# Scores of two attention branches: the second precision pass on 64 rows per head, heads paired on row halves and banks

## The chip, the cores and the metric

The kernel runs on one core of a Trainium2 chip. The metric is the time of one execution on the device in microseconds (us), as a median over runs. Durations inside the kernel come from one profiled execution.

## What is computed

One layer of a hybrid backbone for 256 prompt tokens and 1024 latent tokens on a 16 x 64 grid. A combined projection feeds two attention branches, whose outputs are gated, projected, merged and projected again. Cut to what the change touches:

```python
# branch A: 8 heads x 64, neighbourhood window 8 x 16 on the grid, learned bias, plus 512 context keys
s_nb  = jnp.einsum('brjqhd,brjkhd->brjhqk', qg, kb).astype(jnp.float32) * ATTN_SCALE + bias[None]
s_ctx = jnp.einsum('brjqhd,bshd->brjhqs', qg, ck).astype(jnp.float32) * ATTN_SCALE
p = _softmax_f32(jnp.concatenate([s_nb, s_ctx], axis=-1)).astype(v.dtype)
o = (jnp.einsum('brjhqk,brjkhd->brjqhd', p[..., :nk], vb)
     + jnp.einsum('brjhqs,bshd->brjqhd', p[..., nk:], cv))
# branch B: 8 query heads on 2 key heads, window of 128 tokens each way, a sink logit, the same context keys
p = _softmax_f32(jnp.concatenate([s_nb, s_ctx, sink_col], axis=-1))[..., :-1].astype(v.dtype)
```

## The kernel before, in words

**Stages.** First the norm, modulation, keys and values (to about 137 us), then branch A (to about 575 us), branch B (to about 968 us), then the branch and output projections.

**Precision.** Every product of two float32 operands is made from fast float32r matmuls on operands split into a high and a low part: high x high, high x low, low x high. A head has 64 channels and the array has 128 rows, so a score needs two passes. In the first, `q1` holds the high part of the query in both halves of the rows, and `kk` (projected keys) or `kc` (context keys) holds the high part of the key in one half and the low part in the other: one 128-row matmul gives two of the three products. In the second pass, `q2` holds the low part of the query in the half where that head's high key lies (rows 0 to 63 for the first head of a pair, 64 to 127 for the second).

**Steps.** Each branch runs four pairs of heads. A pair has 9 steps, `STEPS`: step 0 for the 256 prompt tokens of both heads, and steps 1 to 8, each with two score tiles `t` of 128 queries against 512 context keys and 2 or 3 blocks of 128 near keys (2 at the first and last tile of the grid, 3 within; "edge" and "interior" below). In branch B the tiles of a step are the same 128 queries for both heads. In branch A before, they are two neighbouring tiles of one head (`tile_of`), four steps for each head; on each tile the kernel multiplies on 128 rows in both passes, with the other half of `q2` set to zero by GpSimd.

**One step.** TensorE writes the scores to `s_ps` (four banks: two for each `t`), VectorE takes minima and adds the bias (`minima`), ScalarE takes the exponentials, VectorE normalises. TensorE then transposes the probabilities in chunks of up to four blocks (`transposes`, into `t_ps`), ScalarE and VectorE split them into high and low parts `pt`, and TensorE weights the values (`weighted`, into `o_ps`): half 0 on the context values `vc`, half 1 on the near values `vw`. The value block is the stationary operand, and the columns that move are the queries. In one step of a single head, both tiles move through one loading of a value block: 256 columns, where both tiles see the block. ScalarE's `low_half` and VectorE's `add_halves` then combine the halves into `ost`.

**Order.** TensorE's order is written out by hand. In turn s of a pair it makes the scores of step s, the near half of `weighted` for step s-2, two transpose chunks of step s-1, one gate projection `unit` (24 matmuls into `d_ps`), the other transposes of s-1, and the context half of `weighted` for s-1.

**Tiling of the array.** The kernel names no tile of the array: a matmul on operands of 64 rows occupies the row half in which its operands lie.

Of the kernel before, what the change touches and what calls it, by code (L numbers as in the profile page):

```python
# [41 lines left out]
P = 128  # L42
# [32 lines left out]
CHUNKS = {"a": [2] + [4] * SAMPLES, "b": [2, 3] + [4] * (SAMPLES - 2) + [3]}  # L75
NCHUNK = {b: sum(n) for b, n in CHUNKS.items()}
CHUNKS_ALL = PAIRS * (NCHUNK["a"] + NCHUNK["b"])

# [631 lines left out]
def pairs(nc, io, block, hm, ident, wt, wraw, craw, w_in, w_hi, w_lo, tiles, own, counts, earlier_stage, branch, f=None):  # L710
# [61 lines left out]
    if A:  # L772
        comb_in = [sem("comb_in0"), sem("comb_in1")]
        ko_done, ko_out, q2_zero = (sem(n) for n in ("ko_done", "ko_out", "q2_zero"))
# [14 lines left out]

    chunks = CHUNKS[branch]  # L790
    chunk0 = [sum(chunks[:s]) for s in range(STEPS)]

    def chunk_base(p):

        return (0 if A else PAIRS * NCHUNK["a"]) + p * NCHUNK[branch]

# [10 lines left out]
    def tile_of(s, t):  # L807

        return 2 * ((s - 1) % 4) + t if A else s - 1

    def near0(s, t):

        return max(tile_of(s, t) - 1, 0)

    def near_n(s, t):

        return min(tile_of(s, t) + 2, BLOCKS) - near0(s, t)

    def near_bank(s, t):
        w = near_n(s, t) * P  # L820
        return s_ps[:, 2 * t, PAST - w:PAST] if s % 2 else s_ps[:, 2 * t + 1, 0:w]

    def scores_run(s, t):

        w = near_n(s, t) * P
# [3 lines left out]
    def probs_run(s, t):  # L829
        w = near_n(s, t) * P  # L830
# [10 lines left out]
    def probs_block(s, t, kb):  # L841

        c0 = NB + kb * P if kb < 4 or s % 2 == 0 else NB + (kb - 4 - near_n(s, t)) * P
        return pr[:, t, c0:c0 + P]

    def shared(s):

        ends = [(near0(s, t), near0(s, t) + near_n(s, t)) for t in range(2)]
        return [(b, [t for t in range(2) if ends[t][0] <= b < ends[t][1]]) for b in range(ends[0][0], ends[1][1])]

    def chunk_blocks(s):
# [5 lines left out]
        near = [(4 + b - near0(s, t), t) for b, ts in shared(s) for t in ts]  # L857
# [17 lines left out]
    def _(sp):  # L875
# [6 lines left out]
        def body(p, last):  # L882
# [22 lines left out]
            def load_bias(h):  # L905
# [14 lines left out]
            if A:  # L920
                for done, count in stored:
                    sp.wait_ge(done, count)
                load_bias(0)
                load_bias(1)
# [25 lines left out]

    @block.gpsimd
    def _(pool):
        if not A:
            return
        for done, count in stored:
            pool.wait_ge(done, count)
        for h in range(2):
            r1 = HD * (1 - h)
            pool.memset(q2[r1:r1 + HD, h, :].bitcast(F32), 0.0).then_inc(q2_zero, 1)
            pool.wait_ge(q2_zero, h + 1)  # L960

    @block.tensor
    def _(pe):
        def body(p, last):
# [29 lines left out]
            def score(s, t, out, rhs, head=None):  # L994

                if s == 0:
                    h, q0 = head, LAT + t * P
                elif A:
                    h, q0 = (s - 1) // 4, tile_of(s, t) * P
                else:  # L1000
                    h, q0 = t, tile_of(s, t) * P
                cols = lambda ap: ap[..., q0:q0 + P]
                pe.matmul(out, cols(q1[:, h, :]), rhs(h, slice(0, P)), start=True, stop=False)  # L1003
                return pe.matmul(out, cols(q2[:, h, :]), rhs(h, slice(0, P)), start=False, stop=True)  # L1004

            def scores(s):
                if s == 0:
                    if A:
                        pe.wait_ge(q2_zero, 2)
# [12 lines left out]
                for t in range(2):  # L1022
                    if s == 0:
                        for head in range(2):
                            mm = score(s, t, prompt_scores(t, head), lambda h, r: kk[r, h, LAT:TOK], head)
                        continue
                    score(s, t, s_ps[:, 2 * t + s % 2, :], lambda h, r: kc[r, h, :])
                    near = slice(near0(s, t) * P, (near0(s, t) + near_n(s, t)) * P)
                    mm = score(s, t, near_bank(s, t), lambda h, r: kk[r, h, near])
                mm.then_inc(s_done, 1)  # L1030

            def transposes(s, c):

                n = chunk0[s] + c
# [8 lines left out]
            def weighted(s, half):  # L1043
# [5 lines left out]
                last_chunk = chunks[s] if half else 2  # L1049
                pe.wait_ge(lo_done, chunk_base(p) + chunk0[s] + last_chunk)  # L1050
# [8 lines left out]
                elif half == 0:  # L1059
                    h = (s - 1) // 4 if A else 0  # L1060
                    work = [(vc[:, kb, h, :], 2 * kb, 0, 2) for kb in range(4)]
                else:
                    h = (s - 1) // 4 if A else 0
                    work, b0 = [], 8
                    for b, ts in shared(s):
                        work.append((vw[:, b, h * P:(h + 1) * P], b0, ts[0], len(ts)))
                        b0 += len(ts)
# [15 lines left out]
            for s in range(STEPS + 1):  # L1083
# [6 lines left out]
                if s > 0:  # L1090
                    for c in range(min(2, chunks[s - 1])):
# [5 lines left out]
                if s > 0:  # L1097
                    for c in range(2, chunks[s - 1]):
# [7 lines left out]
    def _(act):  # L1106
# [6 lines left out]
        def body(p, last):  # L1113
# [45 lines left out]
            def high(s, chunks):  # L1159

                for c in chunks:
                    n = chunk0[s] + c
# [10 lines left out]
            def exps(s):  # L1173
                for t in range(2):
                    n = pb * 2 * STEPS + 2 * s + t + 1
                    act.wait_ge(m_done, n)
                    if t == 0:

                        act.wait_ge(t_done, chunk_base(p) + (chunk0[s - 1] + min(2, chunks[s - 1]) if s > 0 else 0))
                        act.wait_ge(r_done, pb * STEPS + s)  # L1180
                    if s == 0:
                        for h in range(2):
                            c = 2 * t + h
# [75 lines left out]
            for s in range(STEPS + 1):  # L1259
# [4 lines left out]
                if s > 0:  # L1264
                    high(s - 1, range(min(2, chunks[s - 1])))
# [6 lines left out]
                if s > 0:  # L1272
                    high(s - 1, range(2, chunks[s - 1]))
# [29 lines left out]
    def _(dve):  # L1303
# [7 lines left out]
        def body(p, last):  # L1311
# [83 lines left out]
            def low(s, chunks):  # L1395

                for c in chunks:
                    n = chunk0[s] + c
# [5 lines left out]
            def minima(s):  # L1404
# [4 lines left out]
                if A:  # L1409
                    h = (s - 1) // 4  # L1410
                    dve.wait_ge(comb_in[h], (p + 1) * 16)
# [8 lines left out]
                for t in range(2):  # L1420
                    b = tile_of(s, t)
                    if A:
                        c0 = 0 if 0 < b < BLOCKS - 1 else NB if b == 0 else NB + EDGE
                        near = comb[:, h, c0:c0 + near_n(s, t) * P]
                    else:
                        c0 = P if b == 0 else 0
                        near = band[:, c0:c0 + near_n(s, t) * P]
# [4 lines left out]
            def prompt_minima():  # L1432
# [4 lines left out]
                both = s_ps[:, :, :].rearrange("p (t b) (h c) -> p t b h c", b=2, h=2)[:, :, 0, :, :]  # L1437
                grid4 = lambda ap: ap[:, :].rearrange("p (t h) -> p t h", h=2)
# [6 lines left out]
                sk = nsk[:, :].rearrange("p (o h) -> p o h", o=1).to_broadcast([P, 2, 2])  # L1445
                dve.tensor_tensor(grid4(mx), grid4(mn), sk, ALU.min).then_inc(m_done, 2)

            def normalise(s):
# [13 lines left out]
                for t in range(2):  # L1462
                    if s == 0:
                        for h in range(2):
                            c = 2 * t + h
# [25 lines left out]
            def add_halves(s):  # L1491
# [10 lines left out]
                elif A:  # L1502
                    h, j = (s - 1) // 4, (s - 1) % 4
                    dst = grid(ost[HD * h:HD * h + HD, :], 0, ROWS, 2 * CW * j, 2 * CW).rearrange("p r (t c) -> p t r c", t=2)
                    dve.tensor_tensor(dst, o_ps[0:HD, 0:2 * P].rearrange("p (t r c) -> p t r c", t=2, c=CW),
# [625 lines left out]
```

## Time and profile before

| | |
|---|---|
| median of 3 runs | 1214.7 us (1214.63 to 1215.92) |
| the profiled execution | 1216.12 us, its span 1214.3 us |
| TensorE (PE) busy | 1188.0 us, 98% of the span |
| VectorE (DVE), ScalarE (ACT), GpSimd (POOL) busy | 817.1, 599.9 and 92.9 us |
| granted TensorE clock, mean | 0.997 |

PE stands for TensorE's matmuls and PEld for its weight loads, which run beside them. A matmul's recorded length goes past the moment at which the next may start; the distance from one start to the next is what it costs in a stream. A row of several matmuls gives the first start and the length to the last end. "x128" is a count of instructions, `128*128` the active rows and columns of the array, and `128x256` partitions by moving columns. In this trace `L1003` and `L1004` are the first and second pass of the scores, `L1070` is `weighted`, `L1040` the transposes, `L84` the split projections.

### The profile page before, as it was taken

Reading aid. Unit: us, or ns where it says so; the run is one execution under the profiler, and the core shown is the slowest. Engines: PE = TensorE matmul, PEld = TensorE weight load, DVE = VectorE, ACT = ScalarE, POOL = GpSimd, SP = SyncE. Lnnn points to the kernel's source line nnn. Section 1 sums busy time; section 2 is a strip of 40 time slices with the busy share of each in tenths; the row PEclk is TensorE's granted clock in tenths of the full one; section 3 lists DMA queues with packets and bytes.
Section 4 is the critical chain, followed back from the end, with each engine's and each line's share of the span. In section 5 each row is a group of like instructions: output and inputs, shape, how many; then the busy total and the mean of one; then the engine's idle time right before and its main releaser. Section 6 shows DMA issues by size and latency. Waiting matters only on the chain.

```text
span 1214.3 us, 19600 instructions
## 1 busy us (share of the span) xinstructions
PE 1188.0 (98%) x7408; PEld 1075.5 (89%) x7408; DVE 817.1 (67%) x1588; ACT 599.9 (49%) x1200; POOL 92.9 (8%) x108
## 2 busy tenths in 40 slices
PE   7999999999999999999999999999999999999997
PEld 1799889989998999899899899989989988998995
DVE  4769458656765776587687687688779876354352
ACT  4632335535552654365465455556547675344341
POOL 0000000000000000000000000000000034533430
PEclk9999999999999999999999999999999999999999
DMA  9447702141123215022411111411113376642630
GB/s 362 171 180 225 239 22 72 45 135 61 40 80 95 64 40 159 25 72 77 130 63 47 49 64 39 133 39 58 42 39 121 118 245 193 216 158 76 219 127 35
DMA packets 71617, 132.80 MB, mean 109 GB/s; under 512 B 6758, under 2 KB 47718, under 8 KB 71532
## 3 DMA queue, kind: packets, MB, share of 16 engines
q1 hardware_dynamic: 57420, 109.96, 28.0%
q10 hardware_dynamic: 14112, 21.70, 4.9%
q8 instruction: 54, 0.88, 0.3%
q14 instruction: 31, 0.25, 0.1%
HBM read 96.24 MB, written 35.40 MB: 108 GB/s over the span
## 4 chain that ended last, share of the span: by engine, by line
PE 85%; DVE 9%; ACT 3%; issue 2%; DMA 1%; POOL 0%; ACTq 0%; SPq 0%; DVEq 0%
PE d_ps_pairs L84 23%; PE s_ps_pairs L84 12%; PE y_ps L1858 9%; PE b_ps L84 9%; PE o_ps_pairs L1070 9%; PE t_ps_pairs L1040 7%; PE v_ps L84 6%; PE s_ps_pairs L1004 4%; PE s_ps_pairs L1003 4%; DMA wada<-in_w_ada 1%; DVE pt L1401 1%; PE k_ps L352 1%; DVE mn L1407 1%; DVE q L1392 1%; PE t_ps L344 1%
## 5 line engine op out<-in xcount | busy, mean ns | idle before, releaser
L84 PE MATMUL d_ps_pairs<-h,wt 128*128 128x384 f32 (+2 forms) x1920 | 352.2, 338 | 0.9 <-ACT craw L1212 0.9
L84 PEld LDWEIGHTS d_ps_pairs<-h,wt 128*128 128x128 f32 x1920 | 316.7, 189 | 16.4 <-ACT craw L1212 1.9
L1401 DVE TENSOR_TENSOR pt<-t_ps_pairs,pt 128x512 fp32r<-128x512 f32 (+2 forms) x264 | 152.9, 619 | 64.7 <-ACT pt L1170 63.4
L84 PE MATMUL s_ps_pairs<-h,wt 128*128 128x512 f32 (+1 forms) x864 | 168.2, 354 | 0.0
L84 PEld LDWEIGHTS s_ps_pairs<-h,wt 128*128 128x128 f32 x864 | 141.6, 189 | 21.7
L1170 ACT ACTIVATE pt<-t_ps_pairs 128x512 fp32r<-128x512 f32 (+2 forms) x264 | 130.2, 544 | 16.9 <-PE t_ps_pairs L1040 11.5
L1194 ACT ACTIVATE pr<-s_ps_pairs,mx 128x896 f32<-128x896 f32 (+1 forms) x128 | 125.1, 982 | 26.9 <-DVE mx L1429 26.5
L1040 PE MATMUL t_ps_pairs<-ident_sb,pr 128*128 128x128 f32 x928 | 125.6, 274 | 1.9 <-DVE pt L1401 1.1
L1858 PE MATMUL y_ps<-wo,mg 128*128 128x512 f32 x480 | 113.2, 396 | 0.0
L1040 PEld LDWEIGHTS t_ps_pairs<-ident_sb,pr 128*128 128x128 f32 x928 | 105.4, 140 | 8.7 <-DVE pt L1401 5.7
L1858 PEld LDWEIGHTS y_ps<-wo,mg 128*128 128x128 f32 x480 | 90.0, 188 | 21.6 <-POOL mg L1815 0.2
L1407 DVE TENSOR_REDUCE mn<-s_ps_pairs 128x2 f32<-128x1024 f32 x64 | 78.1, 1221 | 39.5 <-PE s_ps_pairs L1004 39.4
L1812 POOL TENSOR_TENSOR tp<-tp 128x256 f32<-128x256 f32 x40 | 33.2, 829 | 889.3 <-DVE tp L1910 888.9
L1212 ACT ACTIVATE craw<-d_ps_pairs 128x384 f32<-128x384 f32 (+2 forms) x80 | 39.2, 489 | 106.1 <-PE d_ps_pairs L84 105.7
L84 PE MATMUL b_ps<-og,wb 128*128 128x256 f32 x720 | 87.7, 282 | 1.6 <-DVE tp L1910 1.6
L84 PEld LDWEIGHTS b_ps<-og,wb 128*128 128x128 f32 x720 | 86.8, 188 | 2.1 <-DVE wb L1587 1.0
L1244 ACT ACTIVATE otmp<-o_ps_pairs 64x256 f32<-64x256 f32 (+1 forms) x72 | 29.2, 406 | 109.1 <-PE o_ps_pairs L1070 108.6
L1470 DVE TENSOR_SCALAR pr<-pr,rden 128x896 f32<-128x896 f32 (+1 forms) x128 | 80.0, 667 | 2.3
L84 PE MATMUL v_ps<-wv,h 128*128 128x320 f32 x456 | 69.6, 310 | 0.0
L84 PEld LDWEIGHTS v_ps<-wv,h 128*128 128x128 f32 x456 | 67.1, 188 | 1.0 <-issue 0.9
L1910 DVE TENSOR_TENSOR tp<-b_ps,gt 128x256 f32<-128x256 f32 x80 | 31.8, 419 | 45.7 <-PE b_ps L84 31.2
L1003 PE MATMUL s_ps_pairs<-kc,q 128*128 128x512 f32 x128 | 50.5, 394 | 0.0
(192 smaller groups left out, 1584.8 us busy)
## 6 DMA issues: line engine op xcount, KB each, us to landing
wraw<-in_w_gate SPq DMA_DIRECT2D x24, 512.0 KB, 3.9
gt<-gates_d SPq DMA_DIRECT2D x40, 256.0 KB, 4.5
gates_d<-craw ACTq DMA_DIRECT2D x48, 192.0 KB, 1.9
v_d<-vst SPq DMA_DIRECT2D x20, 320.0 KB, 4.5
wada<-in_w_ada SPq DMA_DIRECT2D x12, 512.0 KB, 9.6
oz<-gates_d SPq DMA_DIRECT2D x20, 256.0 KB, 4.6
oz<-o_d SPq DMA_DIRECT2D x20, 256.0 KB, 4.2
x_f<-in_x SPq DMA_DIRECT2D x10, 512.0 KB, 6.3
```

Of the source, the lines that this page charges most:

```text
L84: mm = eng.matmul(out, lhs(a, k), rhs(b, k), start=(k == 0 and i == 0), stop=(k == n_k - 1 and i == 2))
L1003: pe.matmul(out, cols(q1[:, h, :]), rhs(h, slice(0, P)), start=True, stop=False)
L1004: return pe.matmul(out, cols(q2[:, h, :]), rhs(h, slice(0, P)), start=False, stop=True)
L1040: mm = pe.transpose(t_ps[:, n % 2, b * P:(b + 1) * P], probs_block(s, t, kb), ident[:, :])
L1070: mm = pe.matmul(o_ps[:, c0 * P:(c0 + nb) * P], v, pt[:, part, b0 * P:(b0 + nb) * P], start=(half == 0 and part == 0 and (n == 0 or (s == ...
L1170: act.activation(pt[:, 0, c * 512:c * 512 + cols], t_ps[:, n % 2, 0:cols], ACT.Copy).then_inc(hi_done, 1)
L1194: act.activation(probs_run(s, t), scores_run(s, t), ACT.Exp, bias=mx[:, t:t + 1], scale=-1.0, accum_out=den[:, t:t + 1]).then_inc(exp_done, 1)
L1212: act.activation(gst[:, u % 2, 0:n], d_ps[:, 0:n], ACT.Copy).then_inc(g_done, 1)
L1401: dve.tensor_tensor(pt[:, 1, c * 512:c * 512 + cols], t_ps[:, n % 2, 0:cols], pt[:, 0, c * 512:c * 512 + cols].bitcast(F32), ALU.subtract) ...
L1407: dve.tensor_reduce(mn[:, 0:2], s_ps[:, :, :].rearrange("p (t b) c -> p t b c", b=2)[:, :, s % 2, :], AX.X, ALU.min).then_inc(m1_done, 1)
L1470: dve.tensor_scalar(probs_run(s, t), probs_run(s, t), rden[:, t:t + 1], None, ALU.mult).then_inc(p_done, 1)
L1858: mm = pe.matmul(y_ps[:, e, n * 512:(n + 1) * 512], mg[:, a, k, e * P:(e + 1) * P], wo[k][:, b, n * 512:(n + 1) * 512], start=(k == 0 and ...
```

## The change

- The second pass of a score is a matmul on 64 rows: the half of `q2` and of the keys in which that head's data lie. The zero fill of `q2` is gone.
- A step of branch A is now one tile of 128 queries for both heads, as in branch B, so `t` is the head in both branches. In a step the first passes of all four products come first, then the four second passes, alternating between the heads, hence between row halves and banks. In step 0 the banks are those of the heads.
- `weighted` of branch A: a step has two heads, each with its own values, so a value block serves 128 columns, not 256. The number of score columns, transposed blocks and weighted columns is unchanged.
- Chunks of branch A are now as those of B (3 in the edge steps, 4 in the others; before, 4 in all, some of one block).
- The bias of both heads comes in one DMA, waited for as one; `add_halves` of branch A is two instructions of 64x128, not one of 64x256; a GpSimd memset of the last stage waits for branch A's first pair.

```diff
-CHUNKS = {"a": [2] + [4] * SAMPLES, "b": [2, 3] + [4] * (SAMPLES - 2) + [3]}
+CHUNKS = [2, 3] + [4] * (SAMPLES - 2) + [3]
...
-    def near0(s, t):
-        return max(tile_of(s, t) - 1, 0)
+    def near0(s):
+        return max(s - 2, 0)
...
-        return s_ps[:, 2 * t, h * PROMPT:(h + 1) * PROMPT]
+        return s_ps[:, 2 * h, t * PROMPT:(t + 1) * PROMPT]
...
-                sp.dma_start(comb[:, h, :], io["bias"][2 * p + h]).then_inc(comb_in[h], 16)
+                sp.dma_start(comb[:, :, :], io["bias"][2 * p:2 * p + 2].rearrange("h p c -> p h c")).then_inc(comb_in, 16)
...
-            pool.memset(q2[r1:r1 + HD, h, :].bitcast(F32), 0.0).then_inc(q2_zero, 1)
...
-                pe.matmul(out, cols(q1[:, h, :]), rhs(h, slice(0, P)), start=True, stop=False)
-                return pe.matmul(out, cols(q2[:, h, :]), rhs(h, slice(0, P)), start=False, stop=True)
+                h, q0 = (head, LAT + t * P) if s == 0 else (t, (s - 1) * P)
+                if part == 0:
+                    return pe.matmul(out, q1[:, h, q0:q0 + P], k[:, h], start=(s > 0 or t == 0), stop=False,
+                                     skip_group_check=(s == 0))
+                r = slice(h * HD, (h + 1) * HD)
+                return pe.matmul(out, q2[r, h, q0:q0 + P], k[r, h], start=False, stop=True, skip_group_check=(s == 0))
...
+                    for part in range(2):
+                        for t in range(2):
+                            score(s, t, s_ps[:, 2 * t + s % 2, :], kc[:, :, :], part)
+                        for t in range(2):
+                            mm = score(s, t, near_bank(s, t), kk[:, :, near], part)
...
-                elif half == 0:
-                    h = (s - 1) // 4 if A else 0
-                    work = [(vc[:, kb, h, :], 2 * kb, 0, 2) for kb in range(4)]
+                elif A:
+                    near = [vw[:, near0(s) + b, :] for b in range(near_n(s))]
+                    both = near if half else [vc[:, kb, :, :].rearrange("p h c -> p (h c)") for kb in range(4)]
+                    work = [(v[:, t * P:(t + 1) * P], 8 * half + 2 * b + t, t, 1) for b, v in enumerate(both) for t in range(2)]
...
+        pool.wait_ge(exp_done, 2 * STEPS)
         pool.memset(epsc[:, 0:1], EPS).then_inc(eps_set, 1)
```

TensorE in branch A, first pair, from the context half of `weighted` of one step to the transposes of the next, before:

```order
L1070 MATMUL o_ps_pairs<-pt,vc_a 128x256 x8
L1003 MATMUL s_ps_pairs<-kc,q 128x512
L1004 MATMUL s_ps_pairs<-kc,q 128x512
L1003 MATMUL s_ps_pairs<-kk,q 128x384
L1004 MATMUL s_ps_pairs<-kk,q 128x384
L1003 MATMUL s_ps_pairs<-kc,q 128x512
L1004 MATMUL s_ps_pairs<-kc,q 128x512
L1003 MATMUL s_ps_pairs<-kk,q 128x256
L1004 MATMUL s_ps_pairs<-kk,q 128x256
L1070 MATMUL o_ps_pairs<-pt,vw_a 128x128 x2
L1070 MATMUL o_ps_pairs<-pt,vw_a 128x256 x4
L1070 MATMUL o_ps_pairs<-pt,vw_a 128x128 x2
```

and the same place now (`L973` is the first pass, `L976` the second, `L1043` is `weighted`; the rows of `L976` are on 64 rows of the array, which this view does not print):

```order
L1043 MATMUL o_ps_pairs<-pt,vc_a 128x128 x16
L973 MATMUL s_ps_pairs<-kc,q 128x512 x2
L973 MATMUL s_ps_pairs<-kk,q 128x384 x2
L976 MATMUL s_ps_pairs<-kc,q 128x512 x2
L976 MATMUL s_ps_pairs<-kk,q 128x384 x2
L1043 MATMUL o_ps_pairs<-pt,vw_a 128x128 x12
```

The second passes moved behind all first passes, and `weighted` went from 16 matmuls to 28 in such a step. In branch B, TensorE before:

```order
L1070 MATMUL o_ps_pairs<-pt,vc_b 128x256 x8
L1003 MATMUL s_ps_pairs<-kc,q 128x512
L1004 MATMUL s_ps_pairs<-kc,q 128x512
L1003 MATMUL s_ps_pairs<-kk,q 128x384
L1004 MATMUL s_ps_pairs<-kk,q 128x384
```

and now:

```order
L1043 MATMUL o_ps_pairs<-pt,vc_b 128x256 x8
L973 MATMUL s_ps_pairs<-kc,q 128x512 x2
L973 MATMUL s_ps_pairs<-kk,q 128x384 x2
L976 MATMUL s_ps_pairs<-kc,q 128x512 x2
L976 MATMUL s_ps_pairs<-kk,q 128x384 x2
```

Here only the order of the passes moved (before, the four rows of a tile came twice), and `weighted` is as it was.

## Rows read from the trace of the kernel before

**Rows 1.** The page: busy time by engine, and the chain that ended last

```profile
PE 1188.0 (98%) x7408; PEld 1075.5 (89%) x7408; DVE 817.1 (67%) x1588; ACT 599.9 (49%) x1200; POOL 92.9 (8%) x108
PE 85%; DVE 9%; ACT 3%; issue 2%; DMA 1%; POOL 0%; ACTq 0%; SPq 0%; DVEq 0%
```

**Rows 2.** Windows of branch A and branch B: length, busy by engine, clock, DMA

```profile
137.00:575.00 438.00, 437.05 (x2740) 405.15 (x2740) 297.82 (x569) 213.34 (x436) 2.43 (x3) 1.00 0.24 76
575.00:968.00 393.00, 388.50 (x2450) 359.14 (x2449) 306.50 (x675) 226.16 (x509) 0.00 (x0) 1.00 0.23 72
```

**Rows 3.** Waits of TensorE: for whom, us in total, times, longest

```profile
PE o_ps_pairs L1070 <- DVE ost L1510: 2.1, 4, 0.5
...
PE o_ps_pairs L1070 <- DVE ost L1505: 0.8, 4, 0.2
```

**Rows 4.** Timeline of TensorE, one step of branch A: start, length, work, count

```profile
417.95 1.19 PE L1070 MATMUL o_ps_pairs<-pt,vc_a 128*128 128x256 f32 x8
418.98 0.39 PE L1003 MATMUL s_ps_pairs<-kc,q 128*128 128x512 f32 x1
419.21 0.39 PE L1004 MATMUL s_ps_pairs<-kc,q 128*128 128x512 f32 x1
419.44 0.33 PE L1003 MATMUL s_ps_pairs<-kk,q 128*128 128x384 f32 x1
419.61 0.34 PE L1004 MATMUL s_ps_pairs<-kk,q 128*128 128x384 f32 x1
...
420.25 0.28 PE L1003 MATMUL s_ps_pairs<-kk,q 128*128 128x256 f32 x1
420.37 0.28 PE L1004 MATMUL s_ps_pairs<-kk,q 128*128 128x256 f32 x1
420.48 1.04 PE L1070 MATMUL o_ps_pairs<-pt,vw_a 128*128 128x128 f32 x8
421.36 1.06 PE L1040 MATMUL t_ps_pairs<-ident_sb,pr 128*128 128x128 f32 x8
```

**Rows 5.** The same timeline one step earlier, near half of an edge step

```profile
411.64 0.82 PE L1070 MATMUL o_ps_pairs<-pt,vw_a 128*128 128x256 f32 x6
412.30 1.06 PE L1040 MATMUL t_ps_pairs<-ident_sb,pr 128*128 128x128 f32 x8
```

**Rows 6.** TensorE's groups by shape: count, busy us, mean ns

```profile
L1040 PE MATMUL t_ps_pairs<-ident_sb,pr 128*128 128x128 f32 x928 | 125.6, 274 | 1.9 <-DVE pt L1401 1.1
...
L1004 PE MATMUL s_ps_pairs<-kc,q 128*128 128x512 f32 x128 | 50.4, 394 | 0.0
...
L1004 PE MATMUL s_ps_pairs<-kk,q 128*128 128x384 f32 x96 | 32.5, 338 | 0.0
...
L1004 PE MATMUL s_ps_pairs<-kk,q 128*128 128x256 f32 x64 | 17.0, 282 | 0.0
...
L1070 PE MATMUL o_ps_pairs<-pt,vw_a 128*128 128x128 f32 x96 | 16.9, 257 | 0.0
...
L333 PE MATMUL mod_ps<-ident_sb,h 4*128 4x4 f32 x16 | 1.5, 202 | 0.2 <-DVE h L664 0.2
```

**Rows 7.** Timeline of TensorE where it goes between 128 and 4 rows

```profile
34.42 0.60 PE L344 MATMUL t_ps<-ident_sb,x 128*128 128x128 f32 x4
34.95 0.41 PE L333 MATMUL mod_ps<-ident_sb,h 4*128 4x4 f32 x4
35.58 0.41 PE L333 MATMUL mod_ps<-ident_sb,h 4*128 4x4 f32 x4 [0.22 <-DVE h L664]
35.92 0.66 PE L344 MATMUL t_ps<-ident_sb,x 128*128 128x128 f32 x4
```

**Rows 8.** Window of one branch A step from transposes to transposes: TensorE busy first

```profile
421.36:430.41 9.05, 9.05 (x64) 8.85 (x64) 6.99 (x15) 5.60 (x11) 0.00 (x0) 1.00 0.06 23
```

**Rows 9.** Timeline of VectorE in that step: the normalisation

```profile
425.21 1.22 DVE L1470 TENSOR_SCALAR pr<-pr,rden 128x896 f32<-128x896 f32 x2
```

**Rows 10.** DMA issues: the bias, count, size, median us to landing

```profile
comb_a<-in_bias SPq DMA_DIRECT2D x8, 448.0 KB, 6.5
```

More of the change, by code:

```diff
@@ L74 @@
 SAMPLES = STEPS - 1
-CHUNKS = {"a": [2] + [4] * SAMPLES, "b": [2, 3] + [4] * (SAMPLES - 2) + [3]}
-NCHUNK = {b: sum(n) for b, n in CHUNKS.items()}
-CHUNKS_ALL = PAIRS * (NCHUNK["a"] + NCHUNK["b"])
+CHUNKS = [2, 3] + [4] * (SAMPLES - 2) + [3]
+CHUNK0 = [sum(CHUNKS[:s]) for s in range(STEPS)]
+NCHUNK = sum(CHUNKS)
 def split_mm(eng, out, lhs, rhs, n_k):
@@ L788, in grid @@
         return ap[..., 0:LAT].rearrange("p (r c) -> p r c", c=GRID_W)[:, r0:r0 + nr, c0:c0 + ncol]
-    chunks = CHUNKS[branch]
-    chunk0 = [sum(chunks[:s]) for s in range(STEPS)]
     def chunk_base(p):
-        return (0 if A else PAIRS * NCHUNK["a"]) + p * NCHUNK[branch]
+        return (p + base) * NCHUNK
     def rows(ap, g):
@@ L841, in probs_block @@
     def probs_block(s, t, kb):
-        c0 = NB + kb * P if kb < 4 or s % 2 == 0 else NB + (kb - 4 - near_n(s, t)) * P
+        c0 = NB + kb * P if kb < 4 or s % 2 == 0 else NB + (kb - 4 - near_n(s)) * P
         return pr[:, t, c0:c0 + P]
-    def shared(s):
-        ends = [(near0(s, t), near0(s, t) + near_n(s, t)) for t in range(2)]
-        return [(b, [t for t in range(2) if ends[t][0] <= b < ends[t][1]]) for b in range(ends[0][0], ends[1][1])]
     def chunk_blocks(s):
@@ L856, in chunk_blocks @@
             return [[(2 * h + kb, t) for h in range(2) for t in range(2)] for kb in range(2)]
-        near = [(4 + b - near0(s, t), t) for b, ts in shared(s) for t in ts]
+        near = [(4 + b, t) for b in range(near_n(s)) for t in (0, 1)]
         ctx_ = [(kb, t) for kb in range(4) for t in (0, 1)]
@@ L1021, in scores @@
                     pe.wait_ge(exp_done, pb * 2 * STEPS + 2 * s)
[L1022 to L1029, printed above, removed]
+                near = slice(near0(s) * P, (near0(s) + near_n(s)) * P) if s > 0 else slice(LAT, TOK)
+                if s == 0:
+                    for part in range(2):
+                        for t in range(2):
+                            for head in range(2):
+                                mm = score(s, t, prompt_scores(t, head), kk[:, :, near], part, head)
+                else:
+                    for part in range(2):
+                        for t in range(2):
+                            score(s, t, s_ps[:, 2 * t + s % 2, :], kc[:, :, :], part)
+                        for t in range(2):
+                            mm = score(s, t, near_bank(s, t), kk[:, :, near], part)
                 mm.then_inc(s_done, 1)
             def transposes(s, c):
-                n = chunk0[s] + c
+                n = CHUNK0[s] + c
                 if c == 0:
@@ L1058, in weighted @@
                     work = [(vp[:, kb, 0:P], 4 * kb, 0, 4) for kb in range(2)]
-                elif half == 0:
-                    h = (s - 1) // 4 if A else 0
-                    work = [(vc[:, kb, h, :], 2 * kb, 0, 2) for kb in range(4)]
-                else:
[L1063 to L1067, printed above, removed]
+                elif A:
+                    near = [vw[:, near0(s) + b, :] for b in range(near_n(s))]
+                    both = near if half else [vc[:, kb, :, :].rearrange("p h c -> p (h c)") for kb in range(4)]
+                    work = [(v[:, t * P:(t + 1) * P], 8 * half + 2 * b + t, t, 1) for b, v in enumerate(both) for t in range(2)]
+                else:
+                    near = [vw[:, near0(s) + b, :] for b in range(near_n(s))]
+                    both = near if half else [vc[:, kb, 0, :] for kb in range(4)]
+                    work = [(v, 8 * half + 2 * b, 0, 2) for b, v in enumerate(both)]
                 for n, (v, b0, c0, nb) in enumerate(work):
@@ L1090, in body @@
                 if s > 0:
-                    for c in range(min(2, chunks[s - 1])):
+                    for c in range(min(2, CHUNKS[s - 1])):
                         transposes(s - 1, c)
@@ L1097, in body @@
                 if s > 0:
-                    for c in range(2, chunks[s - 1]):
+                    for c in range(2, CHUNKS[s - 1]):
                         transposes(s - 1, c)
```

96 lines of the change are left out of this document (35 added, 61 removed).

## The prediction

> **What bounds the kernel now.** I read the page's busy times first: TensorE is busy 98% of the span, and 85% of the chain that ended last is its own work [rows 1]. Then the windows of the two branches: TensorE works 437.05 of 438.00 us in A and 388.50 of 393.00 in B, at a granted clock of 1.00, while VectorE has 297.82 and 306.50 us of work [rows 2]. Then its waits: the only ones inside the branches that count are for `ost` at the end of a pair, 2.1 us in B and 0.8 in A [rows 3]. So in both branches the end is set by the sum of TensorE's start-to-start distances. What the change adds there is added to the kernel, and what it takes away is a gain until the chain through VectorE and ScalarE shows. That chain has room: in the step shown TensorE is busy for all 9.05 us [rows 8]; the normalisation ends at 425.21 + 1.22 = 426.43 us [rows 9], and TensorE asks for it at 430.41, 4 us later [rows 8].
>
> **Distances.** A matmul of 512 columns takes 419.44 - 419.21 = 0.23 us of the stream, one of 384 takes 0.17, one of 256 takes 0.12 [rows 4]. One of 128 columns is not half of that: eight transposes last 1.06, the last one 0.27 of it [rows 4, 6], so (1.06 - 0.27) / 7 = 0.113 between starts; other such groups give 0.10 to 0.11. The weighted near values say the same: eight matmuls, four of 128 and four of 256 columns, in 421.36 - 420.48 = 0.88 us [rows 4], less 4 x 0.12 leaves 0.10 for each narrow one. In the edge step, six, of which two are narrow, take 0.66 [rows 5], which leaves 0.09. I take 0.11, with 0.10 and 0.113 as bounds: every matmul brings a load of 128 weight columns, and below 256 moving columns the load seems to be what is seen.
>
> **Branch A's weighted values, TensorE.** Before, each of the 32 steps with samples has a context half of 418.98 - 417.95 = 1.03 us [rows 4] and a near half, 0.88 in half of the steps [rows 4] and 0.66 in the other half [rows 5]: 32 x 1.03 + 16 x 0.88 + 16 x 0.66 = 57.6 us. After, all are narrow: 16 for each context half (512), 12 for a near half in 24 steps and 8 in 8 edge steps (352), 864 in all where there were 480. 864 x 0.11 = 95.0 us. That is **+37.4 us** (+28.8 at 0.10, +40.0 at 0.113). No other work hides it, since TensorE has no gap in these steps [rows 8].
>
> **The second pass, both branches.** Its matmuls are the x128, x96 and x64 groups [rows 6]: 128 x 0.23 + 96 x 0.17 + 64 x 0.12 = 53.4 us. By step: 0.80 us in the 48 interior ones, 0.70 in the 16 edge ones, 0.48 in the 8 prompt steps. On 64 rows a matmul streams as many columns, so alone it costs the same; a gain comes only if the two heads' matmuls, now in different row halves and banks, run at once. No row of this trace has two matmuls on different row halves. The bounds are therefore no overlap, 0, and full overlap: 0.40, 0.35 and 0.24 saved, 48 x 0.40 + 16 x 0.35 + 8 x 0.24 = 26.7 us. Between them I take overlap with one weight load after the other, 0.11 us each as above: the four matmuls then start at 0, 0.11, 0.22 and 0.33 us, and the last ends its stream 0.17 later, 0.50 us for 0.80 (edge 0.45 for 0.70, prompt 0.45 for 0.48). That saves 48 x 0.30 + 16 x 0.25 + 8 x 0.03 = **-18.6 us**.
>
> A rule bears on it: the Trainium skill, TensorE: Matmul & The Clock Gate, Part 3, says that matmuls in different row groups run concurrently and gives 3.07 times the rate for four row tiles at 512 columns. No run here shows it. By that efficiency (0.77 of the ideal) two tiles would save about 17 us of the second pass, an estimate from that page.
>
> **Changing between 128 and 64 rows.** Each of the 72 steps goes from 128 rows to 64 and back, 144 changes. The nearest rows are the 4-row transposes of the modulation [rows 7]. The group at 35.58 has its last matmul at 35.58 + 0.41 - 0.20 = 35.79 (mean length 0.20 [rows 6]). The 128-row group behind it is recorded at 35.92 and lasts 0.66 where the like group at 34.42 lasts 0.60, so it really starts near 35.98, 0.19 after. Normal distances are 0.07 (4 rows) and 0.11 (128), which leaves 0.08 to 0.12 for the change. The other way, from the last matmul of the group at 34.42 (34.75) to 34.95 is 0.20, 0.09 above normal, with a wait beside it. I take 0.11: **+15.8 us**. Bounds: 0, and a full wait, the part of a matmul that now overlaps the next (0.39 - 0.23 = 0.16 [rows 4]) and a load not made ahead (0.11), 0.27 or 39 us.
>
> The Trainium skill, TensorEngine Tiling (Array Packing), Key Properties, says that changing the tiling mode drains TensorE, while changing tiles within a mode does not. Rows 7 agree with some such cost. It is the rule that speaks against this change: a step pays for two drains to pair two rather short products.
>
> **Edits at nothing.** VectorE's second `add_halves` instruction (32 of about 0.2 us in branch A) lies in the 4 us of room. The bias in one DMA: its two transfers land in 6.5 us each [rows 10] and are issued at the end of the pair before, more than 30 us ahead of use, so even both in turn are in time. The same minima and exponentials are taken. The zero fill and the GpSimd wait have nobody behind them. Chunks at the edge: the same 108 blocks a pair. If the room were gone, `add_halves` would cost its 6 us, nothing else.
>
> **Sum.** 37.4 - 18.6 + 15.8 = +34.6 us. On the profiled execution, 1216.1 (span 1214.3), that is 1250.7; the median of the runs is 1.4 lower, so 1249. By stage: in A, 438 us become about 475, of which 37.4 is `weighted` and the rest nearly cancels; in B, 393 stay within 2 us, since an interior step gains 0.30 and pays 0.22.
>
> **The rivals.**
> - *Clean pairs and cheap changes.* The halves overlap fully and a change costs at most 0.04: 37.4 - 26.7 + (0 to 6), 1225 to 1231. For it: weight loads are otherwise hidden behind long matmuls. Against it: rows 7. Chance 0.18.
> - *No real overlap.* The float32r matmuls of two halves run one after the other, so the change doesn't do what it says in the scores, and the row changes are paid: 37.4 + 15.8 to 37.4 + 39, 1268 to 1291. For it: no row shows two matmuls at once. Chance 0.25.
> - *Narrow matmuls are faster than they look, and the kernel ends faster.* The place is `weighted` in branch A. Transposes may be slow for a reason of their own, and the 4-row group goes at 0.07 us with the same 128 weight columns [rows 7]. At 0.06 us, 864 cost 52, which is 6 less than before, and with -18.6 + 15.8 the kernel ends at 1206. With the scores as forecast it decides below (57.6 + 2.8) / 864 = 0.070 us. Against it: the narrow ones in `vw_a` left 0.09 to 0.10. Chance 0.05.
> - *In between*, from 1231 to 1241 or 1259 to 1268: a change at 0.05 or 0.18, pairs partly overlapped, or narrow matmuls at 0.10. Chance 0.12.
>
> On the third: the Trainium skill, TensorE: Matmul & The Clock Gate, Back-to-back issue gap, gives about 81 ns for a sustained pair of load and matmul at 128 columns; by it `weighted` would cost 70 us, an estimate, and the whole about 25 us less than my sum. The measured 0.10 to 0.113 decides against it.
>
> **How the numbers follow.** The forecast, 1241 to 1259, has a chance of 0.40. The range goes from 1225, the floor of clean pairs, to 1276, the part of no overlap in which a change costs up to 0.17: 0.40 + 0.17 + 0.12 + 0.12, about 8 in 10. A measurement of this kernel tells about 0.2% (2.4 us) from no change. Faster is the narrow-matmul rival alone and a combination with clean pairs, 0.06; the same 0.02; slower 0.92.
>
> **What would show it.** In the changed profile: (1) `vc_a` and `vw_a` as 864 matmuls of 128 columns with groups of sixteen in about 1.76 us; 1.0 would mean the third rival. (2) The four second-pass matmuls of an interior step from first start to the next work in 0.50 us plus the changes; two starts within 0.02 us mean clean pairs, 0.23 apart means none. (3) The distance from the last 384-column matmul of the first pass to the first of 64 rows, 0.17 normally, now near 0.28, and the same on the way back. (4) Branch A's stage near 475 us and B's near 393, with no new waits of TensorE above 2 us. The prediction is wrong if B's stage moves by over 5 us either way (then the scores were mis-sized) or if A's moves by under 25.

## The result and the profile after

The changed kernel takes 1256.97 us (median of 4 runs, 1255.74 to 1258.45) where the kernel before takes 1214.78 (1214.63 to 1215.92): ratio 1.0346, 95% interval 1.0328 to 1.0364, 42 us slower. The forecast was 1249, range 1225 to 1276.

The page of the changed kernel, busy times and chain, to be held against [rows 1]:

```profile
PE 1227.8 (98%) x7792; PEld 1088.1 (87%) x7792; DVE 824.3 (66%) x1612; ACT 597.9 (48%) x1192; POOL 90.3 (7%) x106
...
PE 84%; DVE 9%; ACT 3%; issue 2%; DMA 1%; POOL 0%; ACTq 0%; SPq 0%; DVEq 0%
```

TensorE is the bound as before, with 384 more matmuls and 39.8 us more work. Nothing else became one.

Its groups by shape (count, busy us, mean ns), which answer to [rows 6]:

```profile
L1043 PE MATMUL o_ps_pairs<-pt,vc_a 128*128 128x128 f32 x512 | 63.5, 277 | 2.9 <-DVE ost L1480 2.9
...
L1043 PE MATMUL o_ps_pairs<-pt,vw_a 128*128 128x128 f32 x352 | 46.0, 279 | 0.0
...
L976 PE MATMUL s_ps_pairs<-kc,q 64*128 64x512 f32 x128 | 32.0, 495 | 0.0
...
L976 PE MATMUL s_ps_pairs<-kk,q 64*128 64x384 f32 x96 | 16.3, 335 | 0.0
```

The 864 narrow matmuls are there. The second pass on 64 rows is busy 32.0 us on the context keys where it was 50.4, and 16.3 on the near keys where it was 32.5: two matmuls at a time.

The timeline of one interior step of branch A (start, length, work, count), which answers to [rows 4]:

```profile
440.42 1.98 PE L1043 MATMUL o_ps_pairs<-pt,vc_a 128*128 128x128 f32 x16
442.24 0.68 PE L973 MATMUL s_ps_pairs<-kc,q 128*128 128x512 f32 x2
442.76 0.52 PE L973 MATMUL s_ps_pairs<-kk,q 128*128 128x384 f32 x2
443.20 0.50 PE L976 MATMUL s_ps_pairs<-kc,q 64*128 64x512 f32 x2
443.54 0.34 PE L976 MATMUL s_ps_pairs<-kk,q 64*128 64x384 f32 x2
443.81 1.56 PE L1043 MATMUL o_ps_pairs<-pt,vw_a 128*128 128x128 f32 x12
445.20 1.06 PE L1014 MATMUL t_ps_pairs<-ident_sb,pr 128*128 128x128 f32 x8
```

The context half of the weighted values takes 442.24 - 440.42 = 1.82 us where it took 1.03, the near half 1.39 where it took 0.88. Two 64-row matmuls of 512 columns last 0.50 together and two of 384 last 0.34, as long as one: both heads start within 0.01 us. This is clean overlap.

Where the price of the pairing lies is best seen in branch B, whose weighted values did not change. TensorE there in an interior step, matmuls and then weight loads:

```profile
671.36 0.51 PE L973 MATMUL s_ps_pairs<-kk,q 128*128 128x384 f32 x2
671.80 0.50 PE L976 MATMUL s_ps_pairs<-kc,q 64*128 64x512 f32 x2
672.13 0.34 PE L976 MATMUL s_ps_pairs<-kk,q 64*128 64x384 f32 x2
672.40 0.98 PE L1043 MATMUL o_ps_pairs<-pt,vw_b 128*128 128x256 f32 x6
```

```profile
671.14 0.41 PEld L973 LDWEIGHTS s_ps_pairs<-kk,q 128*128 128x128 f32 x2
671.80 0.19 PEld L976 LDWEIGHTS s_ps_pairs<-kc,q 64*128 64x128 f32 x2 [0.25 <-issue]
671.91 0.19 PEld L976 LDWEIGHTS s_ps_pairs<-kk,q 64*128 64x128 f32 x2
672.40 0.77 PEld L1043 LDWEIGHTS o_ps_pairs<-pt,vw_b 128*128 128x128 f32 x6 [0.31 <-issue]
```

The last 128-row matmul starts at 671.36 + 0.51 - 0.34 = 671.53. The first 64-row one is recorded at 671.80 and lasts 0.50 where a 512-column matmul lasts 0.39, so it streams from 671.90: 0.37 after, where 0.17 is normal. The change in costs 0.20. About half of it is the weight load: between matmuls of 128 rows it is made beside the matmul ahead (the two loads of 671.14 to 671.55), here it starts only at 671.80, after 0.25 us without a load. On the way back it is the same: from 672.13 to 672.40, plus 0.10 by which the group of six lasts longer (0.98; six such lasted 0.88 before), 0.37 for 0.17. Between the two pairs there is no loss: 671.90 to 672.13 is 0.23. So an interior step saves 0.40 us by overlap and pays 0.40 for two changes.

A table of the two branches (us), each from the start of its first projection to the start of what follows it, in the timelines of the profiled executions. Before, branch A so taken ends at 583.41 and branch B at 976.67, about 8 us behind the cuts of [rows 2]:

| kernel | A, four pairs | B, four pairs |
|---|---|---|
| before | 446.28 | 393.25 |
| changed | 487.91 | 393.06 |

All of the loss is in branch A: 10.0 us in each of three of its pairs and 11.6 in one. That one holds a dip of the granted clock (pairs 2 to 4: length, busy times, clock 0.99 in the middle row; then the dip alone):

```profile
258.54:380.13 121.59, 120.88 (x798) 109.56 (x798) 77.07 (x150) 53.31 (x108) 0.00 (x0) 1.00 0.22 68
380.13:503.35 123.22, 122.51 (x799) 110.72 (x798) 77.09 (x150) 53.30 (x108) 0.00 (x0) 0.99 0.20 66
503.35:624.91 121.56, 120.85 (x798) 109.51 (x798) 77.09 (x150) 53.31 (x108) 0.00 (x0) 1.00 0.28 87
...
380.13:383.60 3.47, 3.47 (x10) 2.71 (x10) 1.79 (x3) 0.38 (x1) 0.00 (x0) 0.51 0.72 279
```

There TensorE runs at the lower of its two levels, 1.2 GHz, on the first projections of the pair. Ahead of it lies the end of a pair with a wait of 0.71 us, as in the other pairs, which have no dip; why it fell is not shown. The dip costs 1.6 us in this execution, and no other trace of this case has one inside the branches.

The last new thing is a wait. The changed kernel's waits for the combined output, to be held against [rows 3], and the end of a pair in A:

```profile
PE o_ps_pairs L1043 <- DVE ost L1480: 4.9, 8, 0.7
```

```profile
253.12 1.54 PE L1043 MATMUL o_ps_pairs<-pt,vw_a 128*128 128x128 f32 x12
254.49 0.63 PE L1014 MATMUL t_ps_pairs<-ident_sb,pr 128*128 128x128 f32 x4
255.83 1.98 PE L1043 MATMUL o_ps_pairs<-pt,vc_a 128*128 128x128 f32 x16 [0.71 <-DVE ost L1480]
```

Between the near half of step 7 and the context half of step 8 only four transposes are left (five before), while ScalarE copies and VectorE adds the output of step 7: 0.7 us of waiting at each pair end of A where it was 0.2, 2.1 us more in all. Experiments 1 and 3 show how much of that comes from the small edits.

### The profile page after: what moved, and what is told of

It is laid out like the page before. It is cut to its first block, busy times and chain, and to the rows that moved or that the text cites. A ratio compares the mean times of both kernels' runs of the same rounds, so it can differ in the third digit from the quotient of the medians.

```text
span 1255.5 us, 20371 instructions
## 1 busy us (share of the span) xinstructions
PE 1227.8 (98%) x7792; PEld 1088.1 (87%) x7792; DVE 824.3 (66%) x1612; ACT 597.9 (48%) x1192; POOL 90.3 (7%) x106
## 4 chain that ended last, share of the span: by engine, by line
PE 84%; DVE 9%; ACT 3%; issue 2%; DMA 1%; POOL 0%; ACTq 0%; SPq 0%; DVEq 0%
PE d_ps_pairs L84 21%; PE o_ps_pairs L1043 12%; PE s_ps_pairs L84 12%; PE y_ps L1828 9%; PE b_ps L84 9%; PE t_ps_pairs L1014 7%; PE v_ps L84 5%; PE s_ps_pairs L973 4%; PE s_ps_pairs L976 3%; DMA wada<-in_w_ada 1%; DVE mn L1380 1%; PE k_ps L352 1%; ACT pr L1167 1%; DVE pt L1374 1%; DVE q L1365 1%
## 5 line engine op out<-in xcount | busy, mean ns | idle before, releaser
L84 PEld LDWEIGHTS d_ps_pairs<-h,wt 128*128 128x128 f32 x1920 | 316.9, 189 | 15.8 <-ACT craw L1185 1.1
L1374 DVE TENSOR_TENSOR pt<-t_ps_pairs,pt 128x512 fp32r<-128x512 f32 (+1 forms) x256 | 152.6, 635 | 69.1 <-ACT pt L1143 66.4
L84 PE MATMUL s_ps_pairs<-h,wt 128*128 128x512 f32 (+1 forms) x864 | 170.8, 357 | 0.0
L1143 ACT ACTIVATE pt<-t_ps_pairs 128x512 fp32r<-128x512 f32 (+1 forms) x256 | 129.7, 556 | 14.7 <-PE t_ps_pairs L1014 9.3
L1043 PE MATMUL o_ps_pairs<-pt,vc_a 128*128 128x128 f32 x512 | 63.5, 277 | 2.9 <-DVE ost L1480 2.9
L1043 PEld LDWEIGHTS o_ps_pairs<-pt,vc_a 128*128 128x128 f32 x512 | 59.7, 192 | 4.1 <-DVE pt L1374 3.7
```

The source lines that it names most:

```text
L84: mm = eng.matmul(out, lhs(a, k), rhs(b, k), start=(k == 0 and i == 0), stop=(k == n_k - 1 and i == 2))
L1043: mm = pe.matmul(o_ps[:, c0 * P:(c0 + nb) * P], v, pt[:, part, b0 * P:(b0 + nb) * P], start=(half == 0 and part == 0 and (n == 0 or (s == ...
L1143: act.activation(pt[:, 0, c * 512:c * 512 + cols], t_ps[:, n % 2, 0:cols], ACT.Copy).then_inc(hi_done, 1)
L1374: dve.tensor_tensor(pt[:, 1, c * 512:c * 512 + cols], t_ps[:, n % 2, 0:cols], pt[:, 0, c * 512:c * 512 + cols].bitcast(F32), ALU.subtract) ...
```

## The experiments

Ratios are to the kernel before, measured on the same chip. Times of branches and pairs are from the profiled executions, taken as in the table above.

**1. The narrow matmuls alone.** From the kernel before:

```diff
+                if A and s > 0:
+                    work = [(v, b0 + i, c0 + i, 1) for v, b0, c0, nb in work for i in range(nb)]
                 for n, (v, b0, c0, nb) in enumerate(work):
```

> The kernel before, with only the weighted values of branch A cut into matmuls of 128 columns (864 for 480); scores as before. Theory 1 (the narrow matmuls are the loss): 864 at 0.112 us against 57.6 us is +38 to +40 us, so 1253 to 1255. Theory 2 (half of the loss lies in the changes between 128 and 64 rows and in the new order of the scores): +20 us or less, under 1235.

Measured 1254.37 us, ratio 1.0318 (1.0301 to 1.0334). Branch A takes 484.89 us, 9.65 more for each pair, and B 393.34. Theory 1 holds: 38.6 of the 40.0 us that A's four pairs lost come from this alone, 0.8 of them as waits for the combined output (1.6 us in branch A, 0.8 before).

```profile
PE o_ps_pairs L1072 <- DVE ost L1507: 1.6, 4, 0.4
```

**2. The pairing alone, in branch B.** From the kernel before (the slices `near` and `q` and the end of the branch are left out):

```diff
+                if s > 0 and not A:
...
+                    for part in range(2):
+                        for k, bank in ((lambda r, h: kc[r, h, :], lambda t: s_ps[:, 2 * t + s % 2, :]),
+                                        (lambda r, h: kk[r, h, near], lambda t: near_bank(s, t))):
+                            for t in range(2):
+                                r = slice(t * HD, (t + 1) * HD) if part else slice(0, P)
+                                mm = pe.matmul(bank(t), (q2 if part else q1)[r, t, q], k(r, t), start=(part == 0),
+                                               stop=(part == 1))
...
```

> The kernel before, with the paired second pass on 64 rows only in the 32 sample steps of branch B; its prompt steps and all of branch A as before. Theory 1 (clean overlap saves 0.40 us in a step, and four stalls of 0.1 us take it back): within 1 us of before, 1214 to 1216. Theory 2 (the row changes cost more than the overlap gives): +5 us or more. Theory 3 (the pairing pays and the waits at pair ends hid it): -5 us or more.

Measured 1215.49 us, ratio 0.9996 (0.9987 to 1.0005). B takes 393.15 for 393.25 us. The pairing is worth nothing that can be measured, as theory 1 had it; where the four stalls lie it had wrong (experiments 6 and 10).

**3. The changed kernel without the pairing.**

```diff
-                r = slice(h * HD, (h + 1) * HD)
+                r = slice(0, P)
                 return pe.matmul(out, q2[r, h, q0:q0 + P], k[r, h], start=False, stop=True, skip_group_check=(s == 0))
```

with the zero fill of the other half of `q2` put back.

> The changed kernel with its second pass on 128 rows again (the other half of the query zero), in the same order and places. Theory 1: no overlap and no row changes, so all that remains is the narrow matmuls and the pair ends: within 2 us of the changed kernel, 1255 to 1259. Theory 2 (row changes cost): faster than the changed kernel by over 5 us. Theory 3 (the pairing pays): slower by over 5 us.

Measured 1256.02 us, ratio 1.0327 (1.0312 to 1.0341), within the noise of the changed kernel's 1.0346 (1.0328 to 1.0364). A pair of A takes 121.5 us as with the pairing, B 393.30. From both sides, the pairing changes next to nothing.

In branch A this kernel differs from that of experiment 1 by the order of tiles and passes and by the small edits. Its branch A takes 485.96 us for 484.89, so these cost 1.1 us, 0.27 in a pair. Two things at the end of a pair add up to that: the two `add_halves` instructions there last 0.58 us for 0.42, and the fifth transpose (0.11), now made elsewhere, no longer fills the wait. That these two are the cause is read off the timelines; no run takes them apart.

**4. Twice the columns in the weighted values.** From the changed kernel, outputs spread over `o_ps` and read apart:

```diff
-                    work = [(v[:, t * P:(t + 1) * P], 8 * half + 2 * b + t, t, 1) for b, v in enumerate(both) for t in range(2)]
+                    work = [(v[:, t * P:(t + 1) * P], 8 * half + 2 * b, t, 2) for b, v in enumerate(both) for t in range(2)]
```

> The changed kernel with each weighted matmul of branch A moving 256 columns (both heads' queries through one head's values, the other head's half of the result not used): the same 864 matmuls and weight loads, twice the columns. Theory 1 (a narrow matmul costs its weight load): 0.118 for 0.112 us, so +5 us, 1262. Theory 2 (a narrow matmul costs by its columns plus a fixed part): 128 more columns at 0.45 ns are 0.06 us each, +50 us.

Measured 1263.43 us, ratio 1.0391 (1.0375 to 1.0408), 5 to 6 us above the changed kernel by the ratios; in the profiled executions branch A takes 7.6 us more (493.89 for 487.91 less the dip). Sixteen matmuls of 256 columns:

```profile
441.38 2.16 PE L1043 MATMUL o_ps_pairs<-pt,vc_a 128*128 128x256 f32 x16
443.37 0.63 PE L973 MATMUL s_ps_pairs<-kc,q 128*128 128x512 f32 x2
```

take 443.37 - 441.38 = 1.99 us, 0.12 each, where sixteen of 128 took 1.82, 0.11 each. Doubling the columns costs a tenth, so the price of a narrow matmul is not in its columns. What else each one brings is a load of 128 weight columns, and in the changed kernel the sixteen loads follow each other at (1.86 - 0.19) / 15 = 0.11 us, as the matmuls do:

```profile
440.39 1.86 PEld L1043 LDWEIGHTS o_ps_pairs<-pt,vc_a 128*128 128x128 f32 x16
```

That the load is what sets the price is an inference from this; no run changes the number of weight columns, and one row does not fit: the 4-row group of [rows 7] loads 128 weight columns too and goes at 0.06 to 0.07 us. The Trainium skill, TensorE: Matmul & The Clock Gate, LDWEIGHTS, gives columns / 1.2 ns, 107 ns for 128; the trace agrees (0.11), and not with the 81 ns of its section on the issue gap.

**5. The second passes head by head.** From the changed kernel:

```diff
-                    for part in range(2):
-                        for t in range(2):
-                            score(s, t, s_ps[:, 2 * t + s % 2, :], kc[:, :, :], part)
-                        for t in range(2):
-                            mm = score(s, t, near_bank(s, t), kk[:, :, near], part)
+                    for t in range(2):
+                        score(s, t, s_ps[:, 2 * t + s % 2, :], kc[:, :, :], 0)
+                    for t in range(2):
+                        score(s, t, near_bank(s, t), kk[:, :, near], 0)
+                    for t in range(2):
+                        score(s, t, s_ps[:, 2 * t + s % 2, :], kc[:, :, :], 1)
+                        mm = score(s, t, near_bank(s, t), kk[:, :, near], 1)
```

> The changed kernel with the second passes ordered head by head (context and near keys of the first head, then those of the second): neighbours are mostly in the same row half, the number of row changes stays. Theory 1 (matmuls overlap when neighbours lie in different row halves): only the middle two overlap, so an interior step gets longer by about 0.07 to 0.2 us, +5 to +13 us on the changed kernel. Theory 2 (no gain from overlap, the stalls are all): 0.

Measured 1257.55 us, ratio 1.0345 (1.0329 to 1.0361): no difference, neither 5 nor 13 us. Theory 2's number came, but not its reason, as experiment 9 shows. The order in the program is now context, near, context, near:

```order
L976 MATMUL s_ps_pairs<-kc,q 128x512
L976 MATMUL s_ps_pairs<-kk,q 128x384
L976 MATMUL s_ps_pairs<-kc,q 128x512
L976 MATMUL s_ps_pairs<-kk,q 128x384
```

and the trace has it as before:

```profile
669.83 0.50 PE L976 MATMUL s_ps_pairs<-kc,q 64*128 64x512 f32 x2
670.16 0.34 PE L976 MATMUL s_ps_pairs<-kk,q 64*128 64x384 f32 x2
```

The second head's context matmul, third in the program, starts within 0.01 us of the first, ahead of the second, in all 64 sample steps. Each row half takes its own next matmul.

**6. Four changes of rows in a step, not two.** From the changed kernel:

```diff
                         for t in range(2):
                             score(s, t, s_ps[:, 2 * t + s % 2, :], kc[:, :, :], part)
+                    for part in range(2):
                         for t in range(2):
                             mm = score(s, t, near_bank(s, t), kk[:, :, near], part)
```

> The changed kernel with the second pass of the context keys right behind their first pass, and that of the near keys behind theirs: four changes between 128 and 64 rows in a sample step where there were two. Theory 1 (a change in costs 0.10, a change out 0.19, a next pair 0.10): +0.19 us in each of 64 steps, +12 us. Theory 2 (the stalls are of the pairs, not of the changes): 0 to 2 us.

Measured 1276.96 us, ratio 1.0502 (1.0485 to 1.0518), 19 us over the changed kernel by the ratios. It is the changes that cost, and more than theory 1 said: a pair of A takes 124.63 us for 121.57, 3.06 / 8 = 0.38 us a step for two more changes, 0.19 each. In B a pair grows by 1.6 to 2.4 us only. Its scores get longer by nearly as much as in A, but the rows of the gate projections and transposes get shorter by 3.6 us in all: small waits of TensorE fill up. Most of them lie in the first two steps of a pair, 0.8 us in each pair; the last pair gives back 0.8 more in later steps. The second pair's transposes of step 1, in the changed kernel and here:

```profile
758.35 0.66 PE L1014 MATMUL t_ps_pairs<-ident_sb,pr 128*128 128x128 f32 x4 [0.16 <-DVE pt L1374]
...
772.09 0.60 PE L1015 MATMUL t_ps_pairs<-ident_sb,pr 128*128 128x128 f32 x4
```

TensorE waited there for VectorE's low parts `pt`, and when TensorE itself comes later they are ready.

**7 and 8. The gate projection at the end of a pair.** The last `unit` moved behind the near half of step 7, in the changed kernel (7) and in the one before (8), with ScalarE's order to match:

```diff
-                if s == STEPS:
-                    unit(s)
                 if s > 0:
                     for c in range(min(2, CHUNKS[s - 1])):
                         transposes(s - 1, c)
-                if s < STEPS:
-                    unit(s)
-                else:
+                if s == STEPS:
                     weighted(s - 2, 1)
+                unit(s)
```

> The changed kernel with the last gate projection of a pair moved behind the transposes and the near values of its second-last step, so that it covers the combining of the halves. The waits for the combined output were 4.9 us (0.7 at each pair end of branch A, 0.5 in B). Theory 1: they go, -4 to -5 us. Rival (the next wait in line is for the normalised probabilities of the last step, now needed 3 us earlier): -2 us or less.

> The kernel before with the same move of the last gate projection. Its waits there were 2.9 us, and 1.1 us for the low parts. Theory 1: -2.5 to -4 us, 1211 to 1212. Rival (a new wait for the probabilities in branch B): -1 us or less.

Measured: 7, 1253.29 us, ratio 1.0309 (1.0295 to 1.0323), 4 us less than the changed kernel; 8, 1219.16 us, ratio 1.0026 (1.0016 to 1.0037), slower by a little, clear of the noise. The waits for the combined output are gone in both. A pair of A in the changed kernel gains 0.95 us, one of B loses 0.4; in the kernel before, both lose, 0.3 and 0.45. So in the two branches 7 gains 3.8 - 1.7 = 2 us, the rival's figure. The ratios say 4 to 5, with an interval of nearly 2 us on either side of each, and what lies beyond the 2 us is not explained. The waits of 8 show why:

```profile
PE t_ps_pairs L1040 <- DVE pt L1395: 4.5, 8, 0.8
PE o_ps_pairs L1070 <- DVE pt L1395: 4.0, 8, 0.6
```

The moved projection had covered VectorE's work: the low parts of step 7's last blocks, which free `t_ps` for the transposes of step 8, and later the low parts of step 8 itself. 8.5 us of waits took the place of 4. The rivals were near in kind (they named the probabilities, the profile names the low parts); a loss of 3 us in the kernel before was foreseen by neither.

**9. Both heads in one row half.** From the changed kernel; the second head's scores get the first head's low part:

```diff
                 r = slice(h * HD, (h + 1) * HD)
-                return pe.matmul(out, q2[r, h, q0:q0 + P], k[r, h], start=False, stop=True, skip_group_check=(s == 0))
+                r = slice(0, HD)
+                return pe.matmul(out, q2[r, 0, q0:q0 + P], k[r, 0], start=False, stop=True, skip_group_check=(s == 0))
```

> The changed kernel with the second pass of both heads taken from the first head's row half (the second head's scores get the first head's low part): still 64 rows, the same changes, but both heads in one half of the array. Theory 1 (two row halves run at once, one does not): the overlap is lost, 0.40 us in an interior step, 0.35 at an edge, 0.24 in a prompt step: +27 us on the changed kernel, 1284. Theory 2 (64-row matmuls are simply cheaper, wherever they lie): 0.

Measured 1279.28 us, ratio 1.0524 (1.0506 to 1.0541), about 22 us over the changed kernel. A pair of A takes 124.85 us, 3.28 more; the overlap by the distances is 6 x 0.40 + 2 x 0.35 + 0.24 = 3.34. In B a pair grows by 1.8 to 2.6, as in experiment 6.

```profile
674.30 0.73 PE L977 MATMUL s_ps_pairs<-kc,q 64*128 64x512 f32 x2
674.87 0.51 PE L977 MATMUL s_ps_pairs<-kk,q 64*128 64x384 f32 x2
```

Two matmuls in one half last 0.73 and 0.51, one after the other; in two halves 0.50 and 0.34. So the gain from overlap is real.

**10 and 11. Twice the second pass, paired and on 128 rows.** The sample steps' second-pass matmuls made twice (the low product counts twice), from the changed kernel (10) and from experiment 3 (11):

```diff
-                return pe.matmul(out, q2[r, h, q0:q0 + P], k[r, h], start=False, stop=True, skip_group_check=(s == 0))
+                return pe.matmul(out, q2[r, h, q0:q0 + P], k[r, h], start=False, stop=(s == 0 or part == 2), skip_group_check=(s == 0))
...
-                    for part in range(2):
+                    for part in range(3):
```

> The changed kernel with the four second-pass matmuls of each sample step made twice in a row (the low product is counted twice), still 64 rows in pairs. Theory 1 (a fixed price for going to 64 rows and back, none between pairs): only the streams are added, 0.40 us in an interior step and 0.35 at an edge, +25 us on the changed kernel, 1282. Theory 2 (every pair has a stall of 0.1 us of its own): +37 us, 1294.

> The same doubling with all second passes on 128 rows (the other half of the query zero). The streams add 0.80 and 0.70 us: +50 us on the single 128-row form, 1306, and 24 us more than the doubled pairs: with twice the work between the changes the pairing pays, where with the single work it came out even. If the price of the changes grew with the work, the two doubled kernels would be as close as the single ones.

Measured: 10, 1277.17 us, ratio 1.0504 (1.0486 to 1.0521); 11, 1301.22 us, ratio 1.0701 (1.0683 to 1.0718). With single work the two forms are within 1 us of each other (1256.97, 1256.02); with double work the paired one is 24 us faster. A pair of A: 3.03 us more paired (3.1 by the streams), 6.3 more on 128 rows (6.2). So the price of the changes is fixed, and none lies between pairs:

```profile
665.57 0.50 PE L976 MATMUL s_ps_pairs<-kc,q 64*128 64x512 f32 x2
665.91 0.34 PE L976 MATMUL s_ps_pairs<-kk,q 64*128 64x384 f32 x2
666.08 0.40 PE L976 MATMUL s_ps_pairs<-kc,q 64*128 64x512 f32 x2
666.32 0.34 PE L976 MATMUL s_ps_pairs<-kk,q 64*128 64x384 f32 x2
```

The third and fourth pair follow at 0.17 and 0.24 us, the streams' own distances. Both totals came 5 us below what was expected, and again it is branch B that took less.

## Why the prediction was right, point by point

- **What bounds the kernel**: right. TensorE's distances set the time, and in A every term that was moved on it showed in the total, to within 0.1 us a pair. In B small waits took up a part (experiments 6, 9, 10 and 11).
- **Weighted values, +37.4**: right. Experiment 1 measured 38.6, of which 0.8 are waits: 37.8. The 0.11 us read off the transposes held, and it is not a price of columns (experiment 4).
- **Overlap, -18.6**: mis-sized. The weight loads of the two halves do not follow each other; both heads start together (0.01 us), and the full 26.7 is saved. Experiment 9 shows it in A (3.28 of 3.34 us a pair). The estimate from the page was also miscounted: at 0.77 of the ideal two tiles save 53.4 - 53.4 / 1.54 = 18.7 us, not 17.
- **Changes of rows, +15.8**: mis-sized the other way. A change costs 0.19 to 0.20 us, not 0.11, about 28 us for 144. In the nearest rows the matmuls around the change are narrow and pay for their loads anyway, so they showed only the wait; behind long matmuls, whose loads are hidden, the load comes on top. The upper bound of 0.27 had both parts. The third sign misled for the same reason: the recorded distance did come to 0.27 us, near the 0.28 that was forecast, but the first 64-row matmul streams 0.10 later than it is recorded.
- The two errors, 8 and 12 us, cancel: -2.8 was forecast for both terms together, about 0 measured (experiments 2 and 3). That is luck; either error alone would have moved the sum to the edge of the forecast or out of it. B's stage stayed within 0.2 us, as forecast.
- **Edits at nothing**: wrong by 1.1 us (experiment 3 against 1). The chunks at the edge and the second `add_halves` instruction were costed in the middle of a pair, where the cover is 4 us; at its end it is four transposes. The limit of 2 us for new waits was also just passed: 2.1 us in A, of which 0.8 came with the narrow matmuls alone.
- **Stage A near 475 us**: its +37 was right by kind but the stage grew by 41.6: 38.6 with the narrow matmuls, 1.1 with the edits, 0.3 for the pairing's share in A, and 1.6 in the dip of the clock. The window to 575 us had also cut the stage 8 us short.
- The rivals: clean pairs came, cheap changes did not; no overlap and faster narrow matmuls did not come (0.11 us).

No version here beats the kernel before: paired scores in B alone are level with it, and the move of the gate projection costs it 0.26%.

## What to carry to other kernels

A stationary operand that serves two tiles is worth keeping: splitting a 256-column matmul (0.12 us) in two of 128 (0.11 each) nearly doubles its price, as columns saved below 256 save next to nothing here. Pairing two short products on row halves halves their stream, but going there and back cost 0.39 us here, so by these numbers it pays only when the second passes between two changes are longer than 0.8 us in series (in this kernel they are 0.80 and 0.70). So gather them before pairing: with twice the work between the changes, the paired form was 24 us ahead (experiments 10 and 11). A useful kernel that gathers them was not tried. Cost a small edit at the place with the least cover, at the ends of loops, not in the middle.

## What the runs showed of the hardware beyond what was expected

- Matmuls on different row halves are not held to the order of the program among themselves (experiment 5): the third started with the first, before the second. The Trainium skill, TensorE: Matmul & The Clock Gate, Part 3, says matmuls start and end strictly in program order; the trace differs.
- A change between 128 and 64 rows costs 0.19 to 0.20 us each way: 0.10 in which neither load nor stream begins, and a weight load of 0.10 that is made beside nothing.
- Two 64-row matmuls start within 0.01 us of each other, loads included: two loads of 128 columns took the time of one. In one half the second load starts 0.11 us behind the first (experiment 9).
